# Three moves in the order of a one-core encoder kernel: squares at the opening, the first two blocks of a down stage, head norms one block sooner

## The chip, the cores and the metric

The kernel runs on one core of a Trainium2 chip. The metric is the device time of one execution in microseconds (us). The kernel before takes 2714.54 us, the median of three runs (2713.57, 2714.54 and 2715.55).

## The reference

One inference step of a small hybrid encoder: two layers, width 1024, 640 tokens (512 of a prompt, and 8 sequences of 16). Everything is float32. Cut to what the change touches:

```python
for i in range(2):
    x = x + 0.5 * swiglu(rmsnorm(x, norm_g[i, 0]), ffn_w_gu[i, 0], ffn_w_d[i, 0])
    xn = rmsnorm(x, norm_g[i, 1])
    y, st = even_mixer(xn, ...) if i % 2 == 0 else odd_mixer(xn, ...)
    x = x + y
    x = x + 0.5 * swiglu(rmsnorm(x, norm_g[i, 2]), ffn_w_gu[i, 1], ffn_w_d[i, 1])
    xg = rmsnorm(x, norm_g[i, 3])
    x = x + (p[i] @ w_ple[i]) * jax.nn.sigmoid(xg @ w_ple_gate[i])
y = rmsnorm(x, final_norm)

def rmsnorm(x, g):
    return x * lax.rsqrt(jnp.mean(x * x, axis=-1, keepdims=True) + EPS) * g
def swiglu(x, w_gu, w_d):               # D_FF = 2816 = 22 blocks of 128
    a, b = jnp.split(x @ w_gu, 2, axis=-1)
    return (jax.nn.silu(a) * b) @ w_d
# even_mixer, of its projection xn @ w_in: the first 12 blocks of 128 columns are q, k, v of the
# delta rule; each of the 4 heads of q and of k is divided by its own norm:
q_a = l2norm(q_a.reshape(B, T, H_A, DK_A)) * (DK_A ** -0.5)
k_a = l2norm(k_a.reshape(B, T, H_A, DK_A))
```

## The kernel before, in words

Activations lie transposed: `x[:, q, :]` is feature block q (128 partitions) by 640 tokens, q = 0 to 7. Every float32 operand of a product is split in a high part (a cast to fp32r) and a low part (what the cast lost), and a product is the sum of three matmuls: high by high (line 913), low by high (914), high by low weights (917). One weight block (`mm`, from line 897) gives 128 output features for 640 tokens. It takes k steps, 8 where the input is 1024 wide; a k step is six matmuls of 128x320. In the feed-forward stages most blocks are computed in pairs (`mm_pair`, lines 928 to 930), by seven half products of sums of the tokens (`tau`) and of the weights (`wsum`).

TensorE (PE) writes each job into one of four PSUM slots, given out in the order of the jobs. VectorE (DVE), or ScalarE (ACT), must have read the slot before the fourth job after it may begin (`slot_free`).

A weight block comes to PE in four steps: SyncE's DMA brings it as float32 (`raw`), ScalarE casts it (`whi`, line 1607, function `prep`; line 1618 for pairs), GpSimd (POOL) subtracts (`wlo`, line 861; VectorE for pairs, line 2197), PE waits for `lo_ready` (or `pair_lo`). On ScalarE the casts stand in a written order among its other work, two blocks ahead of PE; so the cast of a later block waits behind whatever ScalarE waits for. The copies lie in small rings, so a cast also waits until PE has finished the block that lay there.

The stages, each a list of jobs that all engines walk in the same order: load (the opening), six rounds of gate-up and down (each feed-forward is cut in three parts of 8, 8 and 6 hidden blocks, so its last down stage has 6 k steps a block), the projection of the even mixer, its core, its output projection, again feed-forward, the per-layer embedding, and the second layer in the same way with the odd mixer.

**Opening.** x comes by DMA as rows and is transposed by PE. In a loop over q, VectorE copies it (line 2723), ScalarE multiplies by the norm's weight and casts (`x_high`, line 1650), VectorE makes the low part (`x_low`, line 2269), and PE does k step q of the first two blocks of gate-up. Inside that loop VectorE also makes the token sums that the pairs need (`tau_back`, `tau_sums`, lines 2228 to 2235: four instructions each; `tau_rest`, line 2244, follows once ScalarE has cast the sums, line 1647). Behind the loop come the squares (ScalarE, line 1813), one add for each (`square_sum`, lines 2278 and 2280), and then PE's sum over the partitions (`norm_job`, line 968), which stands on PE after the third block. ScalarE's root (line 1732) and VectorE's reciprocal (line 2366, 4 us) follow; `copied_gate`, `copied_hidden` and `plain_gate` multiply the outputs of the first blocks by it and free the slots. Then come the weight sums and low parts of the first pair.

**A down stage.** Its input is the hidden activation, whose last block comes through VectorE's `hf` and `hl` (line 2793) just before it. PE does eight blocks of output. After each, VectorE multiplies by the norm factor (`mul`, line 2181, reads PSUM) and adds into x (line 2919); in the last part of a feed-forward ScalarE then squares x (line 1659), casts it (1650) and casts a weight block, and VectorE adds the square (2280) and makes the low part (2269) for the next stage. ScalarE waits for VectorE's x before it gets to the next weight cast.

**Head norms.** In the second half of the even projection (12 blocks, b = 0 to 11) the eight q and k heads get their norms: ScalarE squares head q (1739), PE sums it over the partitions (968), ScalarE takes the root (1747), VectorE the reciprocal (2373) and multiplies (2374). Head 0 is due at b = HN_LAG = 4. Beside it VectorE does five row steps (`resets`, `decay_rows`, `forget_rows`, `maximum_rows`, `key_rows`, at b = 0 to 4), small operations on 4 partitions for the gates' decays.

## Time and profile before

| | us |
|---|---|
| median of three runs | 2714.54 |
| lowest, highest | 2713.57, 2715.55 |
| the profiled execution, its own time | 2713.01 |
| its span | 2711.3 |
| PE busy | 2652.8 (98%) |
| VectorE busy | 1863.9 (69%) |
| ScalarE busy | 1075.4 (40%) |
| GpSimd busy | 524.6 (19%) |

The span is the time from the first to the last recorded instruction; the execution's own time is 1.7 us more. PE is busy for all but a few microseconds of each stage, so what an edit is worth is read from PE's idle time: where it stood, for what, and what else was late there. In the rows, the number in square brackets is the time for which an engine was idle before an instruction and what released it. The mean granted clock of TensorE over the profiled execution was 0.991 of full speed.

### The profile page before, as it was taken

How to read it: one execution, taken by the hardware profiler on the slowest of the kernel's cores; microseconds unless marked ns; L12 is line 12 of the kernel's file. 1: busy time of each engine (PE TensorE's matmuls, PEld its weight loads, DVE VectorE, ACT ScalarE, POOL GpSimd, SP SyncE). 2: the span in 40 equal slices, each digit the busy share in tenths (PEclk: the TensorE clock that was granted, in tenths of full speed). 3: DMA queues.
4: the chain of work that ended last, by engine and by line, in shares of the span. 5: the costliest groups of instructions: out<-in, count | busy, mean ns of one | idle time of the engine just before them, and what ended most of it. 6: DMA issues, size and time to landing. Idle time of an engine off the chain costs nothing.

```text
span 2711.3 us, 43605 instructions
## 1 busy us (share of the span) xinstructions
PE 2652.8 (98%) x18155; PEld 2613.9 (96%) x18155; DVE 1863.9 (69%) x2188; ACT 1075.4 (40%) x1565; POOL 524.6 (19%) x249
## 2 busy tenths in 40 slices
PE   7999999999999999999999999999999999999998
PEld 7999999999998799999999999999999999999998
DVE  7748386988667768576577874847666786584756
ACT  5525254233222645344244552524411254252545
POOL 1030303232010030201113302030333311102041
PEclk9999999999999999999999999999999999999999
DMA  4323223232003122323232232232222223232231
GB/s 122 86 71 89 83 75 90 55 81 55 17 9 86 54 72 78 94 78 94 63 88 70 71 101 71 78 94 75 83 78 79 63 78 94 63 95 65 82 101 50
DMA packets 401180, 205.57 MB, mean 76 GB/s; under 512 B 15586, under 2 KB 398971, under 8 KB 400984
## 3 DMA queue, kind: packets, MB, share of 16 engines
q1 hardware_dynamic: 400778, 202.70, 26.4%
q8 instruction: 144, 2.36, 0.4%
q14 instruction: 52, 0.43, 0.1%
q10 hardware_dynamic: 206, 0.08, 0.0%
HBM read 195.14 MB, written 7.60 MB: 75 GB/s over the span
## 4 chain that ended last, share of the span: by engine, by line
PE 54%; DVE 9%; ACT 2%; issue 1%; POOL 0%; DVEq 0%; ACTq 0%
PE ps L928 9%; PE ps L930 9%; PE ps L929 9%; PE ps L913 9%; PE ps L917 8%; PE ps L914 8%; DVE ut L2181 1%; DVE x L2919 1%; DVE sumsq L2280 1%; DVE r L2366 1%; DVE hf L2787 1%; DVE x L3105 0%; DVE wlo L2197 0%; DVE hl L2269 0%; PE ps L1198 0%
## 5 line engine op out<-in xcount | busy, mean ns | idle before, releaser
L861 POOL TENSOR_TENSOR wlo<-raw,whi 128x1024 fp32r<-128x1024 f32 (+2 forms) x212 | 513.1, 2423 | 2147.0 <-ACT whi L1607 2146.6
L913 PE MATMUL ps<-xh,whi 128*128 128x320 f32 x1520 | 464.0, 313 | 12.1 <-POOL wlo L861 4.7
L914 PE MATMUL ps<-xl,whi 128*128 128x320 f32 x1520 | 458.4, 309 | 0.0
L913 PE MATMUL ps<-hh,whi 128*128 128x320 f32 x1440 | 437.6, 312 | 5.1 <-DVE hl L2793 2.9
L914 PE MATMUL ps<-hl,whi 128*128 128x320 f32 x1440 | 434.8, 310 | 0.0
L928 PE MATMUL ps<-tau_hi,whi 128*128 128x320 f32 x1296 | 401.3, 310 | 2.1 <-DVE wlo L2197 2.0
L929 PE MATMUL ps<-tau_lo,whi 128*128 128x320 f32 x1296 | 400.5, 309 | 0.0
L930 PE MATMUL ps<-tau_hi,wlo 128*128 128x320 f32 x1296 | 400.5, 309 | 0.0
L1607 ACT CAST whi<-raw 128x1024 fp32r<-128x1024 f32 (+2 forms) x214 | 206.7, 967 | 395.0 <-PE ps L917 355.6
L917 PE MATMUL ps<-xh,wlo 128*128 128x320 f32 x1520 | 347.1, 310 | 0.0
L917 PE MATMUL ps<-hh,wlo 128*128 128x320 f32 x1440 | 329.1, 310 | 0.0
L2181 DVE TENSOR_TENSOR ut<-ps,r 128x640 f32<-128x640 f32 x112 | 92.4, 825 | 328.0 <-PE ps L917 327.0
L913 PEld LDWEIGHTS ps<-xh,whi 128*128 128x128 f32 x1520 | 286.3, 188 | 18.5 <-issue 11.0
L914 PEld LDWEIGHTS ps<-xl,whi 128*128 128x128 f32 x1520 | 286.3, 188 | 0.9 <-issue 0.2
L1618 ACT CAST whi<-raw 128x512 fp32r<-128x512 f32 (+1 forms) x243 | 185.0, 766 | 246.9 <-PE ps L930 125.6
L913 PEld LDWEIGHTS ps<-hh,whi 128*128 128x128 f32 x1440 | 271.4, 189 | 8.1 <-DVE hl L2793 4.5
L914 PEld LDWEIGHTS ps<-hl,whi 128*128 128x128 f32 x1440 | 271.3, 188 | 0.4
L917 PEld LDWEIGHTS ps<-xh,wlo 128*128 128x128 f32 x1520 | 254.7, 188 | 0.0
L928 PEld LDWEIGHTS ps<-tau_hi,whi 128*128 128x128 f32 x1296 | 243.2, 188 | 4.5 <-issue 3.9
L929 PEld LDWEIGHTS ps<-tau_lo,whi 128*128 128x128 f32 x1296 | 243.3, 188 | 0.0
L930 PEld LDWEIGHTS ps<-tau_hi,wlo 128*128 128x128 f32 x1296 | 243.3, 188 | 0.0
L917 PEld LDWEIGHTS ps<-hh,wlo 128*128 128x128 f32 x1440 | 241.4, 188 | 0.0
(433 smaller groups left out, 4829.4 us busy)
## 6 DMA issues: line engine op xcount, KB each, us to landing
raw<-in_ffn_w_gu SPq DMA_DIRECT2D x324, 256.0 KB, 3.9
raw<-in_ffn_w_d SPq DMA_DIRECT2D x64, 512.0 KB, 4.0
raw<-in_w_in_even SPq DMA_DIRECT2D x32, 512.0 KB, 4.1
raw<-in_ffn_w_d SPq DMA_DIRECT2D x32, 384.0 KB, 3.6
raw<-in_w_in_odd SPq DMA_DIRECT2D x24, 512.0 KB, 3.7
raw<-in_w_ple_gate SPq DMA_DIRECT2D x16, 512.0 KB, 3.9
raw<-in_ffn_w_gu SPq DMA_DIRECT2D x14, 512.0 KB, 4.6
raw<-in_w_out_even SPq DMA_DIRECT2D x8, 512.0 KB, 4.0
```

The costliest lines, as they stand in the source:

```text
L861: pool.tensor_tensor(ring(wlo, n), raw[:, slot, 0:kt, :], ring(whi, n).bitcast(fp32), ALU.subtract).then_inc(lo_ready, 1)
L913: pe.matmul(ps[j % 4][:, c, 0:HT], wh[:, k], hi[:, k, cs], start=(k == 0), stop=False)
L914: pe.matmul(ps[j % 4][:, c, 0:HT], wh[:, k], lo[:, k, cs], start=False, stop=False)
L917: last = pe.matmul(ps[j % 4][:, c, 0:HT], wl[:, k], hi[:, k, cs], start=False, stop=(k == kt - 1))
L928: pe.matmul(out, whi[:, w], hi(i), start=(start and i == 0), stop=False, skip_group_check=True)
L929: pe.matmul(out, whi[:, w], lo(i), start=False, stop=False, skip_group_check=True)
L930: last = pe.matmul(out, wlo[:, w], hi(i), start=False, stop=(i == KH - 1), skip_group_check=True)
L1607: act.copy(ring(whi, n), raw[:, raw_pos["block", n], 0:kt, :]).then_inc(hi_ready, 1)
L1618: act.copy(group_ring(whi, g), group_raw(p, g)).then_inc(pair_hi, 1)
L2181: o1(dve.tensor_tensor(out, a, b, ALU.mult))
L2280: own(dve.tensor_tensor(sumsq[:], sumsq[:], src, ALU.add).then_inc(sm, 1), sm)
L2366: o1(dve.reciprocal(r[:], r[:]))
```

## The change

Three independent moves; the arithmetic is the same.

1. Opening. The squares of x are made inside the loop, two steps behind it on ScalarE; VectorE adds five of the eight inside the loop (from step 3 on) and three behind it. The token sums 0, 1 and 2, of which VectorE made all three inside the loop, now follow the last square sum; ScalarE's copy of the first two outputs and its weight cast `prep(3)` stand behind all squares. In the gate-up stage that follows, `tau_rest(1)` moves from ahead of the reciprocal to behind `copied_gate`, and the token sum 3 from ahead of `copied_hidden` to behind `plain_gate(1)`.
2. Down stages with fewer than 8 k steps (the last of each of the four feed-forwards): PE takes k steps 0 to 4 of the first block, 0 to 4 of the second, then the sixth of the first and the sixth of the second.
3. HN_LAG is 3: each head norm stands one block sooner on PE, ScalarE and VectorE. The row steps stay where they are.

```diff
--- before.py
+++ after.py
@@ -457,7 +457,7 @@
         gcol0 = 4 * HA * P
         bcol = [gcol0 + 2 * HA + q * HB * P for q in range(4)]
         icol = bcol[3] + HB * P
-        HN_LAG = NA - 2 * HA
+        HN_LAG = NA - 2 * HA - 1
         s = dict(kind="even_in", n0=len(blocks), prod=prod - 1, pos=[], l2=[], side=side(prod - 1))
         for q in range(3):
             for h in range(HA):
@@ -472,7 +472,7 @@
                 blk((w_in, bcol[q] + h * P), KD, "plain")
                 s["pos"].append([8, 12, 20][q] + h)
 
-                if q * HB + h >= HN_LAG:
+                if HN_LAG <= q * HB + h < HN_LAG + 2 * HA:
                     s["l2"].append(job("hn"))
         stages.append(s)
         Z_ORDER = [0, 1, 2, 4, 3, 5, 6, 7]
@@ -1516,8 +1516,15 @@
                 elif kind == "down":
                     if s.get("split"):
                         first_blocks(s)
+                    hidden = (h_ready, s["hbase"])
+                    both = s["kt"] < KD
+                    if both:
+                        for part in ((0, s["kt"] - 1), (s["kt"] - 1, s["kt"])):
+                            for o in range(2):
+                                mm(s["n0"] + o, *s["hid"], first=hidden, part=part)
                     for o in range(2 if s.get("split") else 0, KD):
-                        mm(s["n0"] + o, *s["hid"], first=(h_ready, s["hbase"]) if o == 0 else None)
+                        if not both or o > 1:
+                            mm(s["n0"] + o, *s["hid"], first=hidden if o == 0 else None)
                         if o == 1 and "pT" in s:
 
                             pe.wait_ge(p_loaded, 32 * (s["layer"] + 1))
@@ -1536,7 +1543,7 @@
                         tposes(j, [((b - first) // 4, b % 4 * P, cacoll[:, b, :]) for b in range(first, last)])
                     for b in range(NA):
                         mm(n + NA + 1 + b, *s["side"])
-                        if b >= HN_LAG:
+                        if HN_LAG <= b < HN_LAG + 2 * HA:
                             q = b - HN_LAG
 
                             pe.wait_ge(hn_sq, s["hn0"] + q + 1)
@@ -1781,6 +1788,12 @@
                     act.dma_start(vstage[a:b, 1, :], ins["conv_c_w"][0].rearrange("j (k p) -> (j k) p", p=P)).then_inc(in_loaded[1], 16)
                     act.dma_start(vstage[b:b + HB, 1, :], ins["mlstm_norm_w"][0].rearrange("(k p) -> k p", p=P)).then_inc(in_loaded[1], 16)
                     act.dma_start(vstage[b + HB:b + HB + 1, 1, :], ins["gdn_norm_w"]).then_inc(in_loaded[1], 16)
+                    def square(q):
+                        if q >= 2:
+
+                            act.wait_ge(sq_added, q - 1)
+                        act.activation([qcopy, stt][q % 2][:], x[:, q, :], ACT.Square).then_inc(sq_ready, 1)
+
                     for q, j in enumerate(s["x"]):
 
                         act.wait_ge(job_done, done_at(j))
@@ -1798,6 +1811,8 @@
                         x_high(0, q, 0)
                         if q == 0:
                             prep(1)
+                        if q >= 2:
+                            square(q - 2)
                     prep(2)
 
                     def first_out(n, out):
@@ -1806,16 +1821,11 @@
                         act.wait_ge(job_done, done_at(j))
                         act.copy(halves(out[:]), ps[j % 4][:, :, 0:HT]).then_inc(slot_free[j % 4], 1)
 
-                    for q in range(KD):
-                        if q >= 2:
-
-                            act.wait_ge(sq_added, q - 1)
-                        act.activation([qcopy, stt][q % 2][:], x[:, q, :], ACT.Square).then_inc(sq_ready, 1)
-                        if q == 3:
-                            first_out(0, gt)
-                            prep(3)
-                        if q == 5:
-                            first_out(1, ut)
+                    square(KD - 2)
+                    square(KD - 1)
+                    first_out(0, gt)
+                    prep(3)
+                    first_out(1, ut)
                 elif kind == "gu":
                     p0, count, n0 = s["p0"], s["count"], s["n0"]
 
@@ -1957,14 +1967,15 @@
                         own(act.activation(c, a, ACT.Relu, bias=bias, scale=sgn).then_inc(row_act, 1), row_act)
                     for b in range(NA):
                         q = b - HN_LAG
-                        if q >= 0:
+                        heads_due = 0 <= q < 2 * HA
+                        if heads_due:
                             if q == 0:
 
                                 act.wait_ge(conv_out, NA)
                             head_squares(s, q, s["l2"], qkv[:, q, :])
                         if b >= 2:
                             prep_next(n + NA + 1 + b, 2)
-                        if q >= 0:
+                        if heads_due:
                             head_root(s, q, s["l2"][q], 1.0)
                 elif kind == "core":
                     z0 = s["z0"]
@@ -2744,20 +2755,23 @@
                         if q + 1 < KD:
                             x_rest(q + 1)
                         x_low(0, q, 0)
-                        i = q // 2 - 1
-                        if i >= 0 and q % 2 == 0:
-                            tau_back(i)
-                        elif i >= 0:
-                            tau_sums(0, i, 0)
+                        if q >= 3:
+                            square_sum(0, q - 3)
+                            dve.sem_inc(sq_added, 1)
+                        if q == 5:
+                            tau_back(0)
                     j = s["cs"]
                     done(j)
                     o1(dve.tensor_copy(castate[:].rearrange("p a b -> p (a b)"), ps[j % 4][:, 0, 0:NA * DECB * CA]))
                     o1(dve.tensor_copy(ccstate[:].rearrange("p a b -> p (a b)"), ps[j % 4][:, 1, 0:KD * DECB * CC]))
                     o1(dve.tensor_copy(vec2[:], ps[j % 4][:, 1, KD * DECB * CC:KD * DECB * CC + NV2]))
                     free(j)
-                    for q in range(KD):
+                    for q in range(KD - 3, KD):
                         square_sum(0, q)
                         dve.sem_inc(sq_added, 1)
+                    tau_sums(0, 0, 0)
+                    tau_sums_alone(1)
+                    tau_sums_alone(2)
                 elif kind == "gu":
                     p0, count = s["p0"], s["count"]
 
@@ -2831,12 +2845,12 @@
                     def plain_start():
                         t = s["tau"]
                         tau_rest(t, 0)
-                        tau_rest(t, 1)
                         norm_recip(s)
                         copied_gate()
-                        tau_sums_alone(3)
+                        tau_rest(t, 1)
                         copied_hidden()
                         plain_gate(1)
+                        tau_sums_alone(3)
                         tau_rest(t, 2)
                         hidden_low(0)
                         if s["plain"] > 3:
@@ -3065,7 +3079,7 @@
                         if b < len(row_steps):
                             row_steps[b]()
                         q = b - HN_LAG
-                        if q >= 0:
+                        if 0 <= q < 2 * HA:
                             head_norm(s, q, qkv[:, q, :], float(DK) ** -0.5 if q < HA else 1.0)
                 elif kind == "core":
 
```

VectorE in the opening, first before: the end of the loop over x (`xl` is the low part of a feature block, `tau_row` the token sum), then the copies of the convolution states.

```order
29 L2723 COPY x<-ps 128x128
30 L2269 SCALAR_TENSOR_TENSOR xl<-x,vec_109,xh 128x640
31 L2235 TENSOR_SCALAR xg_back<-x,vec_109 128x320
32 L2269 SCALAR_TENSOR_TENSOR xl<-x,vec_109,xh 128x640
33 L2228 SCALAR_TENSOR_TENSOR tau_row<-x,vec_109,xg_back 128x320
34 L2229 SCALAR_TENSOR_TENSOR tau_row<-x,vec_109,xg_back 128x320
35 L2230 SCALAR_TENSOR_TENSOR tau_row<-x,vneg,tau_row 128x320
36 L2231 SCALAR_TENSOR_TENSOR tau_row<-x,vneg,tau_row 128x320
37 L2754 COPY castate<-ps 128x288
38 L2755 COPY ccstate<-ps 128x128
39 L2756 COPY vec_110<-ps 128x77
40 L2278 COPY sumsq<-qcopy 128x640
```

The same place after the change:

```order
24 L2280 SCALAR_TENSOR_TENSOR xl<-x,vec_109,xh 128x640
25 L2291 TENSOR_TENSOR sumsq<-sumsq,stt 128x640
26 L2280 SCALAR_TENSOR_TENSOR xl<-x,vec_109,xh 128x640
27 L2291 TENSOR_TENSOR sumsq<-sumsq,qcopy 128x640
28 L2765 COPY castate<-ps 128x288
29 L2766 COPY ccstate<-ps 128x128
30 L2767 COPY vec_110<-ps 128x77
31 L2291 TENSOR_TENSOR sumsq<-sumsq,stt 128x640
32 L2291 TENSOR_TENSOR sumsq<-sumsq,qcopy 128x640
33 L2291 TENSOR_TENSOR sumsq<-sumsq,stt 128x640
34 L2239 SCALAR_TENSOR_TENSOR tau_row<-x,vec_109,xg_back 128x320
35 L2240 SCALAR_TENSOR_TENSOR tau_row<-x,vec_109,xg_back 128x320
```

The token sums of the loop have left it, adds of squares (`sumsq`) stand in their place, and the token sums begin behind the last add.

PE at the down stage of the first feed-forward's last part, before: the fifth and sixth k step of the first block, and the second block's first matmul.

```order
2519 L913 MATMUL ps<-hh,whi 128x320 [waits h_ready]
2520 L914 MATMUL ps<-hl,whi 128x320
2521 L913 MATMUL ps<-hh,whi 128x320
2522 L914 MATMUL ps<-hl,whi 128x320
2523 L917 MATMUL ps<-hh,wlo 128x320 x2
2524 L913 MATMUL ps<-hh,whi 128x320 [waits h_ready]
2525 L914 MATMUL ps<-hl,whi 128x320
2526 L913 MATMUL ps<-hh,whi 128x320
2527 L914 MATMUL ps<-hl,whi 128x320
2528 L917 MATMUL ps<-hh,wlo 128x320 x2
2529 L913 MATMUL ps<-hh,whi 128x320 [waits lo_ready,slot_free0]
2530 L914 MATMUL ps<-hl,whi 128x320
```

After:

```order
2519 L913 MATMUL ps<-hh,whi 128x320 [waits h_ready]
2520 L914 MATMUL ps<-hl,whi 128x320
2521 L913 MATMUL ps<-hh,whi 128x320
2522 L914 MATMUL ps<-hl,whi 128x320
2523 L917 MATMUL ps<-hh,wlo 128x320 x2
2524 L913 MATMUL ps<-hh,whi 128x320 [waits h_ready,lo_ready,slot_free0]
2525 L914 MATMUL ps<-hl,whi 128x320
2526 L913 MATMUL ps<-hh,whi 128x320
2527 L914 MATMUL ps<-hl,whi 128x320
2528 L917 MATMUL ps<-hh,wlo 128x320 x2
2529 L913 MATMUL ps<-hh,whi 128x320 [waits h_ready]
2530 L914 MATMUL ps<-hl,whi 128x320
```

Behind the fifth k step of the first block stands now the first of the second block, with its waits for weights and slot; the sixth k step of the first comes only when five k steps of the second are done.

VectorE in the second half of the even projection, before: from the last row of `maximum_rows` (`R_100` from `minr`) over the `mul` of b = 4 and `key_rows` to the first head norm (`inv`).

```order
491 L3051 TENSOR_TENSOR rtmp_74<-rtmp_72,qkv 4x640
492 L3052 COPY R_98<-rtmp_74 4x640
493 L3054 TENSOR_TENSOR R_100<-rtmp_74,R_100 4x512
494 L3054 TENSOR_TENSOR R_100<-rtmp_74,R_100 4x128
495 L2373 RECIPROCAL inv<-root 128x640
496 L2374 SCALAR_TENSOR_TENSOR qkv<-qkv,inv 128x640
497 L2181 TENSOR_TENSOR qkv<-ps,r 128x640
498 L2373 RECIPROCAL inv<-root 128x640
499 L2374 SCALAR_TENSOR_TENSOR qkv<-qkv,inv 128x640
500 L2181 TENSOR_TENSOR qkv<-ps,r 128x640
```

After:

```order
491 L2385 SCALAR_TENSOR_TENSOR qkv<-qkv,inv 128x640
492 L2192 TENSOR_TENSOR qkv<-ps,r 128x640
493 L3064 TENSOR_SCALAR R_100<-qkv 4x640
494 L3065 TENSOR_TENSOR rtmp_74<-rtmp_72,qkv 4x640
495 L3066 COPY R_98<-rtmp_74 4x640
496 L3068 TENSOR_TENSOR R_100<-rtmp_74,R_100 4x512
497 L3068 TENSOR_TENSOR R_100<-rtmp_74,R_100 4x128
498 L2384 RECIPROCAL inv<-root 128x640
499 L2385 SCALAR_TENSOR_TENSOR qkv<-qkv,inv 128x640
500 L2192 TENSOR_TENSOR qkv<-ps,r 128x640
```

The first head norm now stands ahead of the `mul` of b = 4 and of `key_rows`.

## Rows read from the trace of the kernel before

**Rows 1.** The page's first part: busy time by engine.

```profile
PE 2652.8 (98%) x18155; PEld 2613.9 (96%) x18155; DVE 1863.9 (69%) x2188; ACT 1075.4 (40%) x1565; POOL 524.6 (19%) x249
```

**Rows 2.** Windows: us, busy time of PE, PEld, DVE, ACT, POOL, then PEclk, DMA, GB/s.

```profile
43.00:44.00 1.00, 0.00 (x0) 0.00 (x0) 0.85 (x2) 0.74 (x1) 0.00 (x0) 0.97 0.17 30
...
46.00:51.00 5.00, 4.91 (x15) 4.12 (x16) 3.63 (x4) 4.80 (x6) 2.74 (x1) 0.52 0.32 89
...
60.00:120.00 60.00, 60.00 (x411) 60.00 (x410) 50.35 (x56) 32.44 (x46) 0.00 (x0) 1.00 0.25 71
```

**Rows 3.** PE's timeline at six of its waits (start, duration; idle before in brackets).

```profile
46.09 1.44 PE L968 MATMUL ps<-sumsq,one 128*128 128x320 f32 x2 [4.87 <-DVE sumsq L2280]
...
424.82 0.42 PE L913 MATMUL ps<-hh,whi 128*128 128x320 f32 x1 [0.84 <-DVE hl L2793]
...
662.98 1.16 PE L1057 MATMUL ps<-W,qkv 128*128 128x128 f32 x8 [1.70 <-DVE W L2398]
...
1409.18 0.41 PE L913 MATMUL ps<-hh,whi 128*128 128x320 f32 x1 [0.84 <-DVE hl L2793]
...
1919.74 0.41 PE L913 MATMUL ps<-xh,whi 128*128 128x320 f32 x1 [0.84 <-DVE xl L2793]
...
2581.14 0.41 PE L913 MATMUL ps<-xh,whi 128*128 128x320 f32 x1 [1.52 <-DVE xl L2793]
```

**Rows 4.** By source: lines 2181 and 2919, ns min/median/max.

```profile
L2181 DVE TENSOR_TENSOR ut<-ps,r x112: 824/825/825, 140.1 to 2620.5; 128x640 f32<-128x640 f32 x112
...
L2919 DVE SCALAR_TENSOR_TENSOR x<-ut,x x96: 824/826/2885, 141.0 to 2621.5; 128x640 f32<-128x640 f32 x96
```

**Rows 5.** Timeline of the opening, DVE and POOL; last, PE's second product of a pair.

```profile
30.02 2.37 POOL L861 TENSOR_TENSOR wlo<-raw,whi 128x1024 fp32r<-128x1024 f32 x1 [25.35 <-ACT whi L1607]
...
30.14 2.61 DVE L2228 SCALAR_TENSOR_TENSOR tau_row<-x,vec,xg_back 128x320 f32<-128x320 f32 x1
...
36.16 0.49 DVE L2278 COPY sumsq<-qcopy 128x640 f32<-128x640 f32 x1 [0.57 <-DVE vec L2756]
...
45.22 0.83 DVE L2280 TENSOR_TENSOR sumsq<-sumsq,stt 128x640 f32<-128x640 f32 x1
...
50.40 4.15 DVE L2366 RECIPROCAL r<-r 128x640 f32<-128x640 f32 x1 [1.19 <-ACT r L1732]
...
66.86 1.22 DVE L2197 TENSOR_TENSOR wlo<-raw,whi 128x1024 fp32r<-128x1024 f32 x1
...
L928 PE MATMUL ps<-tau_hi,whi x3: 309/309/309, 74.1 to 75.0; 128*128 128x320 f32 x3
```

**Rows 6.** Timeline of the down stage from 424, DVE and POOL.

```profile
427.05 0.83 DVE L2919 SCALAR_TENSOR_TENSOR x<-ut,x 128x640 f32<-128x640 f32 x1
...
438.43 1.38 DVE L2919 SCALAR_TENSOR_TENSOR x<-ut,x 128x640 f32<-128x640 f32 x1
...
442.11 2.04 POOL L861 TENSOR_TENSOR wlo<-raw,whi 128x768 fp32r<-128x768 f32 x1 [2.98 <-ACT whi L1607]
...
443.43 1.39 DVE L2919 SCALAR_TENSOR_TENSOR x<-ut,x 128x640 f32<-128x640 f32 x1
...
467.80 0.89 DVE L2269 SCALAR_TENSOR_TENSOR xl<-x,vec,xh 128x640 fp32r<-128x640 f32 x1
```

**Rows 7.** Timeline of the down stage from 1403, DVE and POOL.

```profile
1425.83 0.82 DVE L2181 TENSOR_TENSOR ut<-ps,r 128x640 f32<-128x640 f32 x1
...
1429.92 2.05 POOL L861 TENSOR_TENSOR wlo<-raw,whi 128x768 fp32r<-128x768 f32 x1 [6.84 <-ACT whi L1607]
```

**Rows 8.** PE behind the last down stage.

```profile
2626.35 0.39 PE L913 MATMUL ps<-xh,whi 128*128 128x320 f32 x1 [0.73 <-POOL wlo L861]
```

**Rows 9.** Timeline of the head norms, DVE and ACT.

```profile
594.76 0.82 DVE L2181 TENSOR_TENSOR qkv<-ps,r 128x640 f32<-128x640 f32 x1
...
604.59 4.15 DVE L2373 RECIPROCAL inv<-root 128x640 f32<-128x640 f32 x1
...
610.60 0.74 ACT L1739 ACTIVATE sq<-qkv 128x640 f32<-128x640 f32 x1
```

## The prediction

> **What bounds the kernel now.** I read the page first: PE is busy for 98% of the span, VectorE for 69% [rows 1]. So only PE's idle time can be won, and whatever makes PE wait anew is lost. The windows give PE's own pace: 411 matmuls in 60 us, 0.146 us each, so a k step of six is 0.88, a block of six k steps 5.28, one of eight 7.04 [rows 2]. Then PE's timeline, for the waits at the three places of the change [rows 3]: 4.87 us at 46.09 for the last square's sum; 0.84, 0.84, 0.84 and 1.52 us before the sixth k step of four down stages, for the low part of the last hidden block; 1.70 us at 662.98 in the even core, which waits for VectorE. Last, VectorE's and GpSimd's timelines there, for what is late next. That decides here: in all three places VectorE (or a chain VectorE, ScalarE, GpSimd, VectorE) is nearly as late as PE.
>
> One thing has to be seen first, since it sets the sizes. VectorE's multiply from PSUM (line 2181) takes 824 to 825 ns in all 112 cases; its add of two SBUF tiles of the same size (line 2919) takes 824 at least and 2885 at most [rows 4]. The stretched ones lie beside GpSimd: the token sum at 30.14 took 2.61 us instead of about 0.55, and ended at 32.75, when GpSimd's subtraction (30.02, 2.37 long) had ended at 32.39 [rows 5]. So a VectorE instruction with two SBUF inputs that meets a GpSimd subtraction ends about 0.4 us or more behind it, and costs up to 2.05 us more. The Trainium skill says why ("SBUF — State Buffer", section "SBUF: two separate sides"): VectorE, when it has two SBUF inputs, and GpSimd share a port pair as an exclusive lock, and the loser blocks for the whole instruction. The trace agrees (0.82 against 2.88 us). With the lock my sum is +10.0; if the two shared without blocking it would be about -7.6, the rival B below.
>
> **Opening.** Removed: PE's wait of 4.87 us, and what it leads to. The granted clock was 0.97 in 43:44 and 0.52 over 46:51 [rows 2], that is the lower level (1.2 GHz) after PE had been idle since 41.22. About 4.6 us of work ran at half speed: 2.3 us lost. Nominal gain 4.87 + 2.3 = 7.2.
> What is late next: VectorE. The loop gets shorter for it by some 1.5 us, and behind it stand three square sums (from the gap 36.16 to 45.22, 9.06 for seven, some 1 us each with its wait), which end at about 35.1; PE asks for them only at 39.5, so it doesn't wait at its norm. But now 12 token-sum instructions follow, 3 x (4 x 0.58 + 0.4) = 8.2, plus 2.05 where they meet GpSimd's next subtraction: to 45.0. Then `tau_rest(0)`, 1.5, meets the one after: from 45.0 to 48.6 with another 2.05. So the reciprocal starts at about 48.6, not 50.40 [rows 5]: VectorE has won only 1.8 of the 7.2. Behind it: 4.15 + 0.86, `tau_rest(1)` 1.52 that had stood ahead of it, `copied_hidden` 0.86, and `plain_gate(1)` frees its slot at about 56.9. PE, with norm 39.5 to 40.6 and two blocks of 7.04, asks for that slot at 54.7: a new wait of 2.25. Then token sum 3 (2.8), `tau_rest`, hidden and weight sums: the pair's first low part starts at about 66.5 (before 66.86, rows 5). PE is there at 56.9 + 7.04 = 64.0 and waits to 67.8: another 3.8. The second product starts at about 72.3 instead of 74.1 [rows 5].
> Gain 1.8. Bounds: 6.7 if GpSimd never stretches VectorE here; a loss of 0.4 if the clock falls in these two waits. I take 1.8, worked out from the rows' own durations.
>
> **Head norms.** Removed: probably the 1.70 us at 662.98, since the last head norm is over one block (7.04 us) earlier. Added, a wait further up. Head norm 0 (4.15 + 0.86 = 5.0, line 2373 and 2374 [rows 9]) now stands ahead of the `mul` of b = 4 and of `key_rows`. VectorE is late just there: it does the `mul` of b = 3 at 594.76, with `maximum_rows` behind it to 598.4. Then 5.0 to 603.5, the `mul`, and `key_rows`, one copy of which meets GpSimd, to 609.7; head norm 1 to 614.7. Only then comes the `mul` that gives head 3 its data, so ScalarE's squares of it, which in the old order at the same head count were done at 610.6 + 0.74 [rows 9] with 1.5 us to spare, end at about 616.5, where PE asks at 613.9: a wait of 2.6 to 2.8. Sum: -1.7 + 2.7 = +1.0. Bounds: -1.4 (no meeting with GpSimd) and +3.2 (with half clock).
>
> **Down stages.** Removed: 0.84 x 3 + 1.52 = 4.04 [rows 3]. Added: the first block now ends five k steps later. In the stage of 424: the old order had it done at 424.82 + 0.88 = 425.70, x(0) (line 2919) from 427.05 to 427.88 [rows 6]. Now PE starts at 424.82 - 0.84 - 4.40 = 419.58, does ten k steps (8.80) and the sixth: 429.26. x(0) ends at 431.44, 3.56 later. What hangs on it: x(q), square, cast of x, cast of a weight block, GpSimd's subtraction, which holds up x(q+1). One round is from the end of one x to that of the next, 439.81 to 444.82 = 5.0 [rows 6]; GpSimd ends at 444.15, x 0.68 later. PE's round is 5.28. So the chain catches up 0.3 a block, and in the last two blocks, where the cast is 1024 wide (some 5.6), it loses that again. Before, the low part of x(7) was done at 468.69 [rows 6] and PE wanted it, in the eighth k step of the next stage's first block, at 424.82 + 0.88 + 7 x 5.28 + 7 x 0.88 = 468.82: no slack. After, about 470.4 against 467.98: a wait of 2.4, net +1.6. The same at 1919, +1.6.
> In the stage of 1403 the third block's weights take the place of the first's in the ring: first block done 1413.6, cast 0.84, subtraction 1.9: ready at 1416.7, PE there at 1415.4, wait 1.3. And x(0) is 3.4 late, into a chain that also has eight casts of the embeddings (4.4 us) before the `mul` at 1425.83; the weights of the sixth block were ready at 1429.92 + 2.05 = 1431.97 [rows 7], PE at 1432.3. After: 1435.4 against 1432.6, wait 2.8. Net -0.84 + 1.3 + 2.8, about +3.4 with rounding. In the stage of 2575: x(0) 2.9 late; PE already waited 0.73 us for weights in the stage behind it [rows 8], so there was no slack and nearly all of it counts: +2.5.
> Sum 1.6 + 1.6 + 3.4 + 2.5 = +9.1. Bounds: +0.5 (GpSimd stretches nothing, chains catch up) and +11.
>
> **Clock.** The wait of 4.87 brought the lower level, those under 2 us didn't. Of the new waits five are 2.3 to 3.8 long. A wait with half clock costs 2.2 more; I take it about once: +1.7 (0 to +9).
>
> **Sum.** -1.8 + 1.0 + 9.1 + 1.7 = +10.0. Against the profiled execution's own time (2713.0) that is 2723.0; the median lies 1.5 above that execution, so 2724.5.
>
> **The rivals.**
> B, faster: VectorE isn't late. If its adds don't wait for GpSimd at the new places (the collisions lie elsewhere because everything has moved), the opening gives 6.7, the head norms 1.4, the down stages cost 0.5: -7.6, 2707. Its point: the last token sum behind the loop ends before 43 instead of at 45. For it: only 3 of 8 sums in the opening need meet. Against: GpSimd starts whenever a cast ends, and line 2919's maximum of 2885 shows that it happens often. A half of it (opening won, down stages lost) gives about +1 to +3, 2716: the case "same".
> C: the waits just go: -7.2 - 4.0 - 1.7 = -13, 2701.5. For it: the waits are real rows. Against: x(0) must come 3.5 us later by plain count, whatever the ports do.
> D: the clock falls at nearly each new wait: +15 and more, 2730. For it: PE's clock had begun to fall in 43:44, 2 us into a wait [rows 2]. Against: none of the waits under 2 us did it.
>
> **How the numbers follow.** Forecast case 0.56, D 0.07, B 0.12, the half of B 0.19, C 0.06. What this measurement can tell from no change is 0.2%, 5.4 us: slower above 2720, faster below 2709. Of the forecast case's chance 0.03 falls below 2720; so slower 0.56 - 0.03 + 0.07 = 0.60, same 0.19 + 0.03 = 0.22, faster 0.12 + 0.06 = 0.18. The range, 2708 to 2730, holds the forecast with its bounds and the half of B, and leaves out C, most of B and the worst of D. The likeliest case's own range is 2718 to 2729.
>
> **What would show it.** Right: the wait at the norm is gone, new waits of 2 to 4 us stand before the sixth block of gate-up and before the first pair, the reciprocal starts near 48.6; in the even projection PE waits for a sum (line 968) of the fourth head; PE waits for the low part of x (line 2269) at the end of the first block of the even and the odd projection, and for GpSimd's weights in the down stages of 1403 and 2575; x(0) of each ends 3 to 3.6 us later relative to PE's start. Wrong: a first product of a pair by 66 or earlier (B in the opening), or down stages of the last part with no wait above 1 us.

## The result, and the profile after

| | before | changed |
|---|---|---|
| median of six runs, us | 2714.06 | 2724.85 |
| lowest, highest | 2709.13, 2721.57 | 2723.20, 2730.66 |
| the profiled execution's own time | 2713.01 | 2724.71 |
| its span | 2711.3 | 2722.9 |

The changed kernel is slower: ratio 1.0047, 95% interval 1.0034 to 1.0060. (The ratio is an estimate over the runs; the quotient of the two medians is 1.0040.) The forecast was 2724.5.

The page's first part for the changed kernel, which answers to [rows 1]:

```profile
PE 2659.1 (98%) x18155; PEld 2620.8 (96%) x18155; DVE 1861.1 (68%) x2188; ACT 1074.0 (39%) x1565; POOL 526.1 (19%) x249
```

PE is busy 6.3 us longer for the same 18155 matmuls, and idle 5.3 us longer (11.6 in all). So the loss has two halves: new waits, and matmuls that took longer.

PE's timeline (start, duration; idle before). These are the waits that the changed kernel has and [rows 3] has not, but the row at 660.73, which was there (1.09):

```profile
58.42 0.47 PE L913 MATMUL ps<-xh,whi 128*128 128x320 f32 x1 [2.86 <-DVEq L2196]
...
69.42 0.38 PE L928 MATMUL ps<-xh,whi 128*128 128x320 f32 x1 [2.16 <-DVE wlo L2208]
...
469.68 0.42 PE L913 MATMUL ps<-xh,whi 128*128 128x320 f32 x1 [1.69 <-DVE xl L2280]
...
617.16 1.34 PE L968 MATMUL ps<-ut,one 128*128 128x320 f32 x4 [2.36 <-ACT ut L1746]
...
660.73 2.02 PE L1051 MATMUL ps<-R,ident 128*128 128x128 f32 x16 [1.21 <-issue]
...
1421.29 0.38 PE L913 MATMUL ps<-hh,whi 128*128 128x320 f32 x1 [0.99 <-POOL wlo L861]
...
1440.03 0.39 PE L913 MATMUL ps<-hh,whi 128*128 128x320 f32 x1 [2.66 <-POOL wlo L861]
...
1973.99 0.42 PE L913 MATMUL ps<-hh,whi 128*128 128x320 f32 x1 [1.69 <-DVE hl L2280]
...
2614.90 0.39 PE L913 MATMUL ps<-xh,whi 128*128 128x320 f32 x1 [2.28 <-POOL wlo L861]
```

The waits of [rows 3] at 46.09, 424.82, 1409.18, 1919.74, 2581.14 and 662.98 are all gone: the three moves do what they were meant to do. In their place stand eight others, 2.86 + 2.16 + 1.69 + 2.36 + 0.99 + 2.66 + 1.69 + 2.28 = 16.7 us, against 10.6 in [rows 3].

The longer matmuls are the clock's. Windows of the changed kernel behind four of these waits (us; PE, PEld, DVE, ACT, POOL busy; granted clock; DMA):

```profile
58.00:62.00 4.00, 3.58 (x14) 3.58 (x15) 3.60 (x7) 1.64 (x3) 0.00 (x0) 0.58 0.00 0
...
617.00:619.00 2.00, 1.83 (x7) 1.52 (x8) 2.00 (x1) 1.05 (x2) 0.88 (x1) 0.86 0.04 8
...
619.00:622.00 3.00, 3.00 (x14) 3.00 (x13) 2.93 (x3) 0.52 (x1) 1.49 (x1) 0.53 0.06 10
...
1440.00:1446.00 6.00, 5.97 (x30) 6.00 (x31) 4.46 (x5) 2.59 (x4) 2.02 (x1) 0.72 0.08 23
...
2614.00:2618.00 4.00, 3.10 (x13) 3.13 (x14) 3.00 (x3) 2.18 (x3) 1.03 (x2) 0.65 0.11 33
```

Some 3.5 us at the lower of the two levels (1.2 GHz) behind each. What is missing from full speed is the loss: 0.42 x 4 = 1.7 at 58; 0.14 x 2 + 0.47 x 3 = 1.7 at 617; 0.28 x 6 = 1.7 at 1440; 0.35 x 4 = 1.4 at 2614, and 0.3 more in the microsecond behind it. That is 6.8 us of PE's work, where the kernel before lost 2.3 at 46.09. Behind the fifth wait over 2 us, 69.42, the clock stayed at 1.00.

The loss at 58 doesn't lengthen the kernel. VectorE works on without a pause over 0.2 us from 50.05 to the low part of the first pair's weights:

```profile
68.04 1.23 DVE L2208 TENSOR_TENSOR wlo<-raw,whi 128x1024 fp32r<-128x1024 f32 x1
```

PE waits for this at 69.42, for 2.16 us. At full speed it would have been there 1.7 us sooner and waited 1.7 us longer (an estimate from these rows). So 5.1 us of the 6.8 count at most.

To compare executions I took the time between rows that every kernel has (for example 486 is the 0.86 us wait for GpSimd at 485.99 in the second block of the even projection) and list the difference from the profile before, in us:

| stretch, by the profile before | changed | changed again | opening alone | down alone | norms alone |
|---|---|---|---|---|---|
| to 349 (opening) | -0.3 | -0.6 | -0.5 | -1.5 | +1.8 |
| 349 to 486 (down stage) | +1.2 | +1.2 | 0.0 | +1.2 | 0.0 |
| 486 to 656 (even projection) | +4.3 | +4.3 | 0.0 | -0.1 | +2.7 |
| 656 to 717 | -2.0 | -2.0 | 0.0 | 0.0 | -2.0 |
| 865 to 961 (sample part of the core) | +1.7 | +2.1 | +2.7 | -1.1 | -3.8 |
| 1333 to 1472 (down stage) | +4.4 | +4.4 | 0.0 | +4.4 | 0.0 |
| 1844 to 2203 (down stage, odd mixer) | +1.2 | +1.2 | +0.2 | +1.2 | 0.0 |
| 2504 to 2636 (down stage) | +2.1 | +2.2 | 0.0 | +2.1 | -0.1 |
| all | +11.6 | +11.8 | +1.8 | +5.6 | -1.9 |

Stretches that are left out differ by 0.4 at most. The changed kernel's two profiles agree within 0.1 in all rows but two. No edit touches the stretch from 865 to 961, and the kernel before has it at two lengths (see the experiment with the same program twice); the edits' part in its +1.7 stays open. Without it the changed kernel is 9.9 us longer than before.

The first row has to be read with care. The order of the opening is the old one in six profiles (before, before again, down alone, norms alone and the two runs with `key_rows` at b = 6 and with the add from PSUM alone), and there it took from 1.5 us less to 1.8 us more than in the profile before. With the move it took 0.3, 0.6 and 0.5 less. On average that is half a microsecond, but each single difference lies within what the old order does by itself.

### The profile page after: what moved, and what is told of

Same layout as the page of the kernel before. It is cut to its first block, busy times and chain, and to the rows that moved or that the text cites. A ratio compares the mean times of both kernels' runs of the same rounds, so it can differ in the third digit from the quotient of the medians.

```text
span 2722.9 us, 43608 instructions
## 1 busy us (share of the span) xinstructions
PE 2659.1 (98%) x18155; PEld 2620.8 (96%) x18155; DVE 1861.1 (68%) x2188; ACT 1074.0 (39%) x1565; POOL 526.1 (19%) x249
## 3 DMA queue, kind: packets, MB, share of 16 engines
q8 instruction: 144, 2.36, 0.4%
## 4 chain that ended last, share of the span: by engine, by line
PE 54%; DVE 9%; ACT 2%; issue 1%; POOL 0%; DVEq 0%; ACTq 0%
PE ps L928 9%; PE ps L929 9%; PE ps L930 9%; PE ps L913 9%; PE ps L917 8%; PE ps L914 8%; DVE x L2933 1%; DVE ut L2192 1%; DVE sumsq L2291 1%; DVE hl L2280 1%; DVE r L2377 1%; PE ps L1198 0%; DVE hf L2801 0%; DVE x L3119 0%; DVE wlo L2208 0%
```

## The experiments

Twelve runs. "Timed" gives medians of the run and of the kernel before on the same chip; the ratio is again an estimate over the runs, not their quotient.

### The three moves apart

The diffs are the hunks of the change: those of the opening, the one of the down stages, those of HN_LAG.

> The kernel before with the opening's move alone. Theory T (VectorE's chain sets the opening; what PE wins at its norm it gives back at two new waits): PE's second product of the first pair starts within 0.5 us of 74.1, near 73.6, with new waits of 2 to 3 us before the sixth block of gate-up (near 58) and before the first pair (near 69), and TensorE's granted clock at the lower level for some 3 to 4 us behind the first of them. The whole -0.4 us, or about 2713.7 against 2714.1. Rival R1 (the moves are worth what PE's wait was, and the other two moves spoil it): second product at 67 to 69, whole -5 to -7 us. The even core behind it should take as long as before; if its stretch at the lower clock (near 890 to 903) is longer here too, that length does not hang on the head norms.

Measured: timed 2714.17 against 2713.40, ratio 1.0000 (0.9988 to 1.0012). PE's timeline:

```profile
58.26 0.63 PE L913 MATMUL ps<-xh,whi 128*128 128x320 f32 x1 [2.86 <-DVEq L2188]
...
69.27 0.38 PE L928 MATMUL ps<-xh,whi 128*128 128x320 f32 x1 [2.17 <-DVE wlo L2200]
...
73.49 0.42 PE L928 MATMUL ps<-tau_hi,whi 128*128 128x320 f32 x1 [0.48 <-ACT sq L1828]
```

Product with token sums at 73.49 (74.1 in [rows 5]), the same two waits as in the changed kernel. The opening's move is worth about half a microsecond, alone as well. In the six profiles with the old order this product starts at 72.56 to 75.87, so a difference as small as this is not beyond doubt. The rival R1 (67 to 69) is out. The core's stretch was not as long as before but 2.7 us longer.

> The kernel before with the order of the first two down blocks alone (four stages with 6 k steps). T (the first x of the stage comes 3.5 us later, and a chain x, square, cast, weight cast, GpSimd's subtraction, x carries that through the stage): +8 us: +1.2 from 424 to 486, +4.4 from 1403 to 1462, +1.2 from 1919 to 1975, +2.1 from 2575 to 2638, with the same waits as in the changed kernel (1.7 for the low part of x in the first block of the even and the odd projection; 1.0 and 2.7 for weights in the stage of 1403; 2.3 in that of 2575). Rival (the added time needs VectorE's delays of the other moves): -4 us, the four waits just gone.

Measured: timed 2721.92 against 2713.40, ratio 1.0029 (1.0018 to 1.0040). By stretch +1.15, +4.35, +1.16, +2.14: the changed kernel's numbers within 0.03, with the lower clock again behind the waits of 2.65 and 2.29 us. The down stages' move costs 8.5 us by the medians, 8.8 by the stretches; it is most of the loss, and needs neither of the others.

> The kernel before with the head norms one block sooner alone. T: PE waits 2.4 us before the sum of the fourth head (near 617), the lower clock for about 3 us behind it, and no longer 1.7 us near 663; the stretch from 486 to 682 +2.2 us. The even core behind 682 as long as before (then its +1.7 us in the changed kernel is not of the head norms), or, rival, +1.7 us here too (then it is).

Measured: timed 2714.33 against 2713.40, ratio 1.0003 (0.9992 to 1.0014). PE's timeline:

```profile
618.05 1.34 PE L968 MATMUL ps<-ut,one 128*128 128x320 f32 x4 [2.35 <-ACT ut L1739]
```

The windows behind the wait:

```profile
618.00:620.00 2.00, 1.95 (x10) 1.64 (x11) 2.00 (x1) 0.93 (x1) 0.99 (x1) 1.00 0.03 8
...
620.00:622.00 2.00, 2.00 (x15) 2.00 (x15) 1.97 (x2) 0.00 (x0) 1.41 (x1) 1.00 0.00 0
```

The wait of 2.35 us is about the changed kernel's (2.36), but here the granted clock stayed at 1.00, where the changed kernel had 0.86 and 0.53. So 486 to 717 is +0.65 and not +2.2: the expected lower clock didn't come. The core's stretch was 3.8 us shorter, not longer; with that of the opening alone (+2.7) neither side of my rival holds.

### What makes PE wait at the head norms

```diff
-                        if b < len(row_steps):
-                            row_steps[b]()
+                        if b < 4 or b == 6:
+                            row_steps[min(b, 4)]()
```

> As the last, but the row step key_rows stands on VectorE at b = 6 instead of b = 4, behind the fourth head norm. T (key_rows between head norm 0 and head norm 1 makes VectorE late for ScalarE's root and squares): head norm 1 ends near 610 instead of 615, PE's wait of 2.4 us is gone, and the gain at 663 stays: the stretch from 486 to 682 is 1.5 to 1.7 us shorter than before, 4 less than with the head norms' move alone. Rival (PE waits since one block is too little time for squares, sum and root in any order): the wait of 2.4 stays.

Measured: timed 2708.61 against 2713.40, ratio 0.9982 (0.9971 to 0.9993). 486 to 717 is -2.0 us; the time fell by more than this stretch and the whole profile (-2.3) show. VectorE's timeline in the changed kernel, from head norm 0's product to head norm 1's:

```profile
603.37 0.82 DVE L2385 SCALAR_TENSOR_TENSOR qkv<-qkv,inv 128x640 f32<-128x640 f32 x1
...
604.23 0.82 DVE L2192 TENSOR_TENSOR qkv<-ps,r 128x640 f32<-128x640 f32 x1
...
607.09 3.12 DVE L3068 TENSOR_TENSOR R<-rtmp,R 4x512 f32<-4x512 f32 x2
...
610.36 4.16 DVE L2384 RECIPROCAL inv<-root 128x640 f32<-128x640 f32 x1
...
614.55 0.82 DVE L2385 SCALAR_TENSOR_TENSOR qkv<-qkv,inv 128x640 f32<-128x640 f32 x1
```

ScalarE's there:

```profile
615.47 0.79 ACT L1754 ACTIVATE root<-ps,eps 128x640 f32<-128x640 f32 x1 [8.58 <-DVE qkv L2385]
...
616.38 0.74 ACT L1746 ACTIVATE ut<-qkv 128x640 f32<-128x640 f32 x1
```

VectorE's with `key_rows` at b = 6:

```profile
602.86 0.82 DVE L2375 SCALAR_TENSOR_TENSOR qkv<-qkv,inv 128x640 f32<-128x640 f32 x1
...
603.72 0.82 DVE L2182 TENSOR_TENSOR qkv<-ps,r 128x640 f32<-128x640 f32 x1
...
604.69 4.15 DVE L2374 RECIPROCAL inv<-root 128x640 f32<-128x640 f32 x1
...
608.88 0.83 DVE L2375 SCALAR_TENSOR_TENSOR qkv<-qkv,inv 128x640 f32<-128x640 f32 x1
```

In the changed kernel `key_rows` stands between 605.20 and 610.2, its adds stretched to 3.12 us beside GpSimd, and head norm 1 ends at 615.37. ScalarE's root (615.47) has waited for exactly this (its row names line 2385), and its squares (616.38 to 617.1) come behind the root; PE starts at 617.16. With `key_rows` elsewhere head norm 1 ends at 609.71, and no wait is left. The rival (one block is too little) is out. Of the 5.0 us of `key_rows` about 2.1 are GpSimd's (an estimate: two adds of the same size took 1.00 us together at 598.15); without them PE's wait would have been some 0.3 us. No run takes them away alone.

### The same program twice

> The kernel before, once more, for its profile. In the profiles so far the stretch from 865 to 961 us of the even core took 95.6 us before, 97.3 in the changed kernel, 98.3 with the opening alone, 94.5 with the down stages alone, 91.8 with the head norms alone. Theory K (that stretch differs from one execution to the next with TensorE's granted clock, and not by the edits): it differs from 95.6 by over 1 us here too, with other windows at the lower clock, while every other stretch agrees within 0.5 us. Rival: 95.6 again, so the edits change it.

Measured: one run, 2709.15 (before on that chip 2713.22). 865 to 961 took 92.0 us instead of 95.6; every other stretch is within 0.13. Theory K holds for the kernel before. The first 19 us of the stretch as a window, and in it the same 24 matmuls in PE's timeline, in the profile before:

```profile
865.00:884.00 19.00, 15.31 (x92) 14.08 (x93) 13.22 (x25) 2.27 (x5) 0.00 (x0) 0.73 0.88 222
...
871.60 5.39 PE L1057 MATMUL ps<-W 128*128 128x128 f32 x24 [0.77 <-ACT W L2059]
```

The same of the second execution:

```profile
865.00:884.00 19.00, 15.43 (x126) 14.31 (x126) 16.61 (x30) 5.83 (x9) 0.00 (x0) 1.00 0.86 223
...
870.06 3.20 PE L1057 MATMUL ps<-W 128*128 128x128 f32 x24 [0.77 <-ACT W L2059]
```

The same 24 matmuls took 5.39 us in the first execution and 3.20 in the second; the granted clock of the window was 0.73 and 1.00. In the fourteen profiles this stretch took from 91.5 to 100.8 us. The timed runs of the kernel before lie in groups, near 2709, 2713 and 2722 us: the two profiled executions, 2713.01 with 95.6 us and 2709.15 with 92.0, belong to the first two. No profile shows what makes the third.

### GpSimd's hold on VectorE in the down stages

```diff
-    mul(halves(ut[:]), P2(j), halves(r[:]))
-    free(j)
-    own(dve.scalar_tensor_tensor(x[:, o, :], ut[:], s["scale"], x[:, o, :], ALU.mult, ALU.add)...)
+    mul(P2(j), P2(j), halves(r[:]))          # only where s["kt"] < KD
+    own(dve.scalar_tensor_tensor(halves(x[:, o, :]), P2(j), s["scale"], halves(x[:, o, :]), ALU.mult, ALU.add)...)
+    free(j)
```

> The down stages' order alone, and in those four stages VectorE writes the scaled block back into PSUM and adds from there, so that the add into x has one SBUF input and not two. Theory L (the add is held by GpSimd's subtraction, and that is what carries the late first x through the stage): no add of line 2931 or so over 0.9 us; the chain's round falls from 5.0 us to about 4; the low part of x(7) is ready before PE asks for it: no wait in the first block of the projections, 424 to 486 0.8 us shorter than before instead of 1.2 longer, the same from 1919; in the stage of 1403 the wait for the third block (ring) stays at about 1.0 less up to 0.9, the 2.7 us wait falls under 1; whole -2 to 0 us against before instead of +8. Rival (the 3.5 us delay itself is too long whatever the ports do): waits of 1.7, 2.7 and 2.3 stay, whole +7 to +8.

Measured, the add by source (ns min/median/max), first in the changed kernel:

```profile
L2933 DVE SCALAR_TENSOR_TENSOR x<-ut,x x96: 824/826/2420, 140.7 to 2633.6; 128x640 f32<-128x640 f32 x96
```

With one input from PSUM, in the four stages:

```profile
L2926 DVE SCALAR_TENSOR_TENSOR x<-ps,x x32: 823/824/826, 429.9 to 2623.5; 128x640 f32<-128x640 f32 x32
```

No add is stretched. The low part of x(7) starts at 465.15, against 468.74 in the changed kernel, and PE doesn't wait for it. By stretch: -0.9, -0.3, -0.9, -0.3 instead of +1.2, +4.4, +1.2, +2.1. The first x is as late as before (its add starts at 429.89, against 430.01 in the changed kernel). So the late first x alone does no harm; it is GpSimd's hold on the add that carried it through the stage (theory L). The Trainium skill's page "SBUF — State Buffer", section "SBUF: two separate sides", names just this case, two SBUF inputs on VectorE against GpSimd, and the runs agree: 2420 against 826 ns. The wait of 2.66 at 1440 is gone, the ring's wait at the third block stays (1.00), as expected; of the 2.28 in the last stage 1.36 stays. The old order with this add was not run, so the 2.4 us by the stretches (below) belong to order and add together, and the order may have no part in them. Timed, though, it is 2713.96 against 2713.22, ratio 1.0000 (0.9989 to 1.0011): in the profile the stages gave those 2.4 us and the stretch from 865 to 961 took 100.7 us, 5.1 more than in the profile before. A second profile with this edit (below) has 100.8. That edit doesn't touch this stretch; whether it brings on the longer time there stays open.

### VectorE relieved in the opening

```diff
 # ScalarE, behind the last square (VectorE's copies and tau_back are left out)
+                    x_back(0, 0, 0)
+                    act.wait_ge(job_done, done_at(s["cs"]))
+                    act.copy(castate...); act.copy(ccstate...); act.copy(vec2...)   # then frees the slot
+                    x_back(0, 2, 0)
 # and x_back(0, 4, 0), x_back(0, 6, 0) behind the first two casts of token sums
```

> The opening's move alone, and beside it VectorE is relieved: its three copies of the convolution states and its four small products for the token sums (line 2235) go to ScalarE, which waits there. T (VectorE's chain sets the opening): the reciprocal starts at 44 to 47 instead of 50.05, the wait before the sixth block of gate-up is gone, PE's second product of the first pair starts at 67 to 70 instead of 73.5; -4 to -6 us against before. Rival (something else is next, PE's slots or ScalarE): not earlier than 72, and -1 us or less.

Measured: timed 2710.31 against 2713.22, ratio 0.9986 (0.9974 to 0.9998). The reciprocal starts at 46.77, the wait before the sixth block is gone, a wait of 3.19 before the first pair is left, and the granted clock falls behind it; the product starts at 71.81. So T's first two points are right; the product (67 to 70 expected) is missed by 1.8 us, and the whole (-4 to -6 expected) is -2.9 by the medians and -2.3 by the stretch to 349. The rival (not earlier than 72) doesn't hold either. The last run, with the same opening and the clock at its upper level, shows what the clock took: from the end of the wait to the product 6.17 us here and 4.23 there.

```diff
 # ScalarE
-                        tau_round(s["tau"], 1); x_back(0, 6, 0); prep(g0 + 4); norm_root(s)
+                        norm_root(s); prep(g0 + 4); tau_round(s["tau"], 1); x_back(0, 6, 0)
 # VectorE, before the first pair
-                            tau_rest(t, 3); plain_hidden(1); pair_low(p0, 0); hidden_low(1)
-                        sums_4(p0); plain_gate(2); pair_low(p0, 1)
+                            plain_hidden(1); pair_low(p0, 0); hidden_low(1)
+                        sums_4(p0); pair_low(p0, 1); tau_rest(t, 3); plain_gate(2)
```

> The opening with VectorE relieved (as in the run before), and two orders changed on top: on ScalarE the root stands ahead of the second cast of token sums; on VectorE the first two weight low parts of the first pair stand ahead of the fourth token low part and the third plain gate. T (PE's wait of 3.2 us before the first pair is VectorE's queue, and with it goes the lower clock): the wait there falls to 0.5 to 2 us, the clock stays at the upper level, the product that started at 71.8 starts at 67 to 69; -5 to -7 us against before. Rival (the wait only moves to the next products): 71 or later, no gain over the run before.

Measured: timed 2713.32 against 2713.23, ratio 1.0003 (0.9990 to 1.0016); the product at 74.90. A miss: the wait before the pair fell to 0.17, but one of 3.14 came at 58.49 and one of 3.67 at 74.90. VectorE, then GpSimd, with the order of the run before:

```profile
43.66 0.55 DVE L2243 SCALAR_TENSOR_TENSOR tau_row<-x,vneg,tau_row 128x320 f32<-128x320 f32 x1
...
44.24 1.49 DVE L2256 TENSOR_TENSOR tau_lo<-tau_row,tau_hi 128x1280 fp32r<-128x1280 f32 x1
...
46.77 4.15 DVE L2378 RECIPROCAL r<-r 128x640 f32<-128x640 f32 x1 [1.04 <-ACT r L1732]
```
```profile
44.64 3.36 POOL L861 TENSOR_TENSOR wlo<-raw,whi 128x1024 fp32r<-128x1024 f32 x1 [4.89 <-ACT whi L1607]
```

The same two with the new order on ScalarE:

```profile
43.88 2.59 DVE L2243 SCALAR_TENSOR_TENSOR tau_row<-x,vneg,tau_row 128x320 f32<-128x320 f32 x1
...
46.51 3.58 DVE L2256 TENSOR_TENSOR tau_lo<-tau_row,tau_hi 128x1280 fp32r<-128x1280 f32 x1
...
50.12 4.15 DVE L2378 RECIPROCAL r<-r 128x640 f32<-128x640 f32 x1
```
```profile
43.41 5.33 POOL L861 TENSOR_TENSOR wlo<-raw,whi 128x1024 fp32r<-128x1024 f32 x2 [3.44 <-ACT whi L1607]
```

The weight cast came 1.25 us earlier on ScalarE, so GpSimd started at 43.41 instead of 44.64. There it caught VectorE's last token sum (2.59 instead of 0.55), and its second subtraction the low part behind it (3.58 instead of 1.49). The reciprocal is 3.35 us later, although its root was there at 42.1, earlier than ever. One cast earlier on a third engine decided this.

The wait of 3.67 before the product is another matter. It ends with a copy on ScalarE that stands behind this row:

```profile
72.76 0.74 ACT L1840 ACTIVATE stt<-gt 128x640 f32<-128x640 f32 x1 [4.66 <-DVE gt L2804]
```

ScalarE waits there for VectorE's third plain gate, which the second of the two new orders has put behind the fourth token low part and the second weight low part. In the run before the same row starts at 67.72. Two orders were changed in one run, and neither was run alone.

### Put together

> All three moves, each with what hid its gain taken away: the opening as in the last kernel, key_rows at b = 6, the add into x from PSUM in the down stages with 6 k steps. If the parts add up: opening -5 to -6, head norms -2.0, down stages -2.4: -9 to -11 us against before, 2702 to 2704. Rival (a part needs VectorE time that another has taken): -6 us or less.

> The same without the down stages' move (their old order, and the add from SBUF): -7 to -8 us against before, 2705 to 2706. If it is as fast as the one with all three, the down stages' move is worth nothing even mended.

Measured: 2714.05 and 2712.56 against 2713.23, ratios 0.9999 (0.9985 to 1.0014) and 0.9999 (0.9982 to 1.0015). Both are misses; both carry the opening with the two new orders. By stretch the first has +2.3 to 349, -0.9 to 486, -2.0 for 656 to 717, -0.3, -0.9 and -0.9 in the other down stages, and 100.8 us from 865 to 961. The parts add up but for the opening.

> The changed kernel once more, for its profile. Theory K (only the stretch from 865 to 961 of the even core differs from one execution to the next; the rest is the edits'): against the profile before, the opening -0.5, the stretch to 486 +1.2, to 656 +4.2 with the lower clock behind the wait near 617, to 1472 +4.4, to 2203 +1.2, to 2636 +2.1 again within 0.3 us; the core's stretch another value than +1.65.

Measured: 2724.80; the numbers are in the table. The core's stretch was 97.7 against 97.3: theory K wanted another value and is not borne out by this pair. What differed in the kernel before (95.6, 92.0) repeated here, and so did the clock's fall: behind the same four of the five waits over 2 us.

> The opening's move with VectorE relieved (as the run that was 2.3 us earlier at the first product with token sums) and the head norms' move with key_rows at b = 6 (2.0 us less), the down stages in their old order. If the two add up: -4.3 us in the profile outside the stretch from 865 to 961, 2706 to 2709 as a median. Rival (the opening's end decides how long the clock stays low in the core, and that eats it, as it did for the down stages with the add from PSUM): 2712 to 2714.

Measured: timed 2707.02 against 2713.75, ratio 0.9982 (0.9971 to 0.9993): faster than both kernels. Outside the stretch from 865 to 961 the profile is 7.0 us shorter, not 4.3: the opening gave 3.9 and not 2.3, since the clock didn't fall, and the norms 1.9; the other 1.2 are small differences elsewhere. The product with token sums starts at 70.10, after the same wait as in the run with this opening alone. PE's row and the window behind it, with this opening alone (first two fences) and then here:

```profile
65.64 0.61 PE L928 MATMUL ps<-xh,whi 128*128 128x320 f32 x1 [3.19 <-DVE wlo L2209]
```
```profile
65.00:71.00 6.00, 5.36 (x20) 5.39 (x21) 5.67 (x7) 3.34 (x5) 0.00 (x0) 0.50 0.00 0
```
```profile
65.87 0.38 PE L928 MATMUL ps<-xh,whi 128*128 128x320 f32 x1 [3.18 <-DVE wlo L2217]
```
```profile
65.00:71.00 6.00, 4.65 (x30) 4.42 (x31) 5.67 (x7) 4.53 (x7) 0.00 (x0) 1.00 0.00 0
```

The same wait within 0.01 us, the lower level behind it in one execution and not in the other.

## Why the prediction was right, and where it was not

The number was right (2724.5, measured 2724.85), the sign and the cause of most of it too: VectorE, or its chain with ScalarE and GpSimd, is as late as PE at all three places, and what PE no longer waits for it waits for a little later. But three terms were mis-sized, and that their errors nearly cancel is luck. All against the profiled executions:

| term | predicted | measured |
|---|---|---|
| opening | -1.8 | -0.3 |
| head norms, without the lower clock | +1.0 | +0.5 |
| down stages, without it | +9.1 | +5.4 |
| lower clock behind new waits, where it counts | +1.7 | +5.1 |
| 865 to 961 | 0 | +1.7 |
| left over | 0 | -0.8 |
| sum | +10.0 | +11.6 |

A second piece of luck: the prediction added 1.5 us, by which the median before lay above the profiled execution. In the changed kernel the median lies 0.1 above it; this makes up for the 1.6 us by which the sum is short.

**Opening.** Right in mechanism: no wait at the norm, new waits of 2.86 and 2.16 (predicted 2.25 and 3.8). The size failed: the reciprocal started at 50.05, not 48.6, the pair's low part at 68.04, not 66.5, the product at 73.64, not 72.3. VectorE, which sets the time here, had won 0.35 us at the reciprocal and not 1.8.

```profile
36.11 2.68 DVE L2239 SCALAR_TENSOR_TENSOR tau_row<-x,vec,xg_back 128x320 f32<-128x320 f32 x1 [0.57 <-DVE sumsq L2291]
...
45.70 2.79 DVE L2242 SCALAR_TENSOR_TENSOR tau_row<-x,vneg,tau_row 128x320 f32<-128x320 f32 x1
...
50.05 4.15 DVE L2377 RECIPROCAL r<-r 128x640 f32<-128x640 f32 x1
```

Two of VectorE's instructions met GpSimd, as counted, but the first at 36.11 (2.68 us) behind square sums that ended at 35.5 and not 35.1, and the second was the last token sum (45.70, 2.79 us), not the low part behind it. The prediction's own sum also slips: 35.1 + 8.2 + 2.05 is 45.35, not 45.0. The wait of 2.16 is 1.6 shorter than predicted since PE came to it late, by the lower clock behind 58.42; for the same reason that clock cost nothing. Two other runs bear this out: behind the wait near 58 the granted clock over 58:65 was 0.76 with the two new orders of the opening and 0.58 in the run put together without the down stages' move, and the product started at 74.90 and 74.67: the run that was longer at the lower level was not later. What the prediction calls the pair's second product is its third, the first with token sums.

**Head norms.** The wait (2.36, predicted 2.6 to 2.8), its place and the gain at 663 (2.0, predicted 1.7) are right. One link was wrong: the squares don't need the `mul` that the prediction names; head q comes from the first half of the projection. They stand on ScalarE behind the root of head 2, which needs head norm 1 out of the way. The time came out right since both follow head norm 1.

**Down stages.** Here the term failed in its size. x(0) ended at 430.83, 2.95 us later than in [rows 6], or 3.3 counted from a PE that is 0.3 early through the opening (predicted 3.56). The waits are the predicted ones: 1.69 and 1.69 for the low part of x (predicted 2.4), 0.99 and 2.66 in the stage of 1403 (1.3 and 2.8), 2.28 before the sixth block of 2575 (no wait was given, only +2.5 for the stage). The first two are less because the low part of x(7) was done at 469.63 and not 470.4. The chain caught up in one step: x(1) was only 0.94 us later than before, since the add of x(1) in the kernel before had itself met GpSimd for longer. In the kernel before, then in the changed one:

```profile
432.33 2.46 DVE L2919 SCALAR_TENSOR_TENSOR x<-ut,x 128x640 f32<-128x640 f32 x1
```
```profile
434.33 1.40 DVE L2933 SCALAR_TENSOR_TENSOR x<-ut,x 128x640 f32<-128x640 f32 x1
```

The stage of 1403 took +4.4 of which 1.7 is the clock, so +2.7 (predicted +3.4). In the last stage I had let nearly all of the 2.9 count (+2.5); the stage took +2.1, of which up to 1.7 is the clock: about half of the term's error is here. Whether it would have been less without the clock no run shows, since PE waited for the same chain behind it (0.59 there, 0.73 in [rows 8]).

**Clock.** The step that failed most: "I take it about once". It fell behind four of the five waits over 2 us in the changed kernel and counted three times; 69.42 (2.16) is the one without. But that isn't a rule either: behind 2.35 us at 618 with the head norms alone it did not fall, nor behind 3.18 us in the last kernel, and behind 3.19 us at the same place it did. What it costs where it counts is read from the norms: 486 to 656 took +2.7 without its fall (norms alone) and +4.3 with it.

**The rivals.** B (the lock doesn't bite) is what the run with the add from PSUM made true for the down stages: the move then gains 2.4 us by the stretches. That is even more than B said (a cost of 0.5), and how much of it is the order's own was not run. The prediction's theory stands on that run. C (waits just go) is wrong in each of the three runs of one move. D came nearer in its mechanism than its chance of 0.07 said (four of five waits), not in its time.

## What to carry to other kernels

Before taking a wait away from the busy engine, list what the engine next to it must still do by the following hand-over. Here all of 10.6 us of waits could go and the kernel lost 10 us, because VectorE had no slack at the same places; moving VectorE's small copies to ScalarE, and one row step behind the norms, turned the same idea, less the down stages, into a gain (ratio 0.9982, 2707.02 against 2713.75). The norms with the row step behind them have the same ratio alone; the opening's 2.3 to 3.9 us stand in the stretches and, alone, in a ratio of 0.9986.

Where GpSimd and VectorE share work on SBUF, an edit on a third engine that starts GpSimd a microsecond earlier can cost VectorE three; reading one operand from PSUM took the add out of that here.

## What the runs showed of the hardware

- A VectorE add of 128x640 with two SBUF inputs took 824 to 2420 ns beside GpSimd's subtractions; the same add with one input in PSUM 823 to 826 ns in all 32 cases, with GpSimd's subtractions in the stage as before.
- TensorE's lower clock level came or did not come behind the same wait of the same instructions (3.19 and 3.18 us; 2.36 and 2.35 us), and took 1.7 us of PE's work each time in the changed kernel, 1.9 us behind the wait of 3.19. Where PE had to wait for VectorE behind it anyway, it cost nothing. A stretch of 96 us of small matmuls took 91.5 to 100.8 us in fourteen profiles, and 95.6 and 92.0 in two of the same program. The times of one kernel's runs spread over 4 to 15 us; a change worth 1 us was seen in the stretches of a profile and not in the times.
